# The opening of a two-layer diffusion backbone: order of its loads, context vectors by TensorE, a narrow low-rank block, squares ahead

## The reference, cut to what matters

```python
mod_x = (sc @ ada_w[l] + ada_b[l])      # sc = silu(c); scc = silu(c_ctx) for the context
sh1x, sc1x, g1x, sh2x, sc2x, g2x = split(mod_x, 6)
hx = modulate(rms_norm(x, norm1_g[l]), sh1x, sc1x)   # h * (1 + scale) + shift
gq, gkk, gv, gg, lr_f, lr_b, bq, bk, bv = split_cols(h @ w_in, EVEN_WIDTHS)
```

## Time and profile before

| | |
|---|---|
| median of three runs | 1530.45 us (1528.8 to 1530.65) |
| profiled execution | 1528.42 us, span 1526.5 us |
| granted TensorE clock, mean | 0.998 |
| TensorE busy | 97% of the span |
| VectorE, ScalarE, GpSimd busy | 66%, 44%, 43% |

### The profile page before, as it was taken

The page is one execution under the profiler, slowest core; times in us unless marked ns, Lnnn a source line. Parts: engine busy times, 40 slices in busy tenths (PEclk is TensorE's granted clock), DMA queues, the critical chain, the costliest instruction groups (busy, mean ns, idle before and its releaser), DMA issues.

```text
span 1526.5 us, 26643 instructions
## 1 busy us (share of the span) xinstructions
PE 1478.6 (97%) x10374; PEld 1265.1 (83%) x10374; DVE 1010.6 (66%) x1534; ACT 679.2 (44%) x1171; POOL 657.7 (43%) x445
## 2 busy tenths in 40 slices
PE   6999999989999999999999999999999999999997
PEld 3888864468898989999898999855568998998996
DVE  4898877569888656466667655767636655456465
ACT  4745325562333424334242544245535464545365
POOL 0031026602556334343434433355645665556472
PEclk9999999999999999999999999999999999999999
DMA  9532110045224233243546211100013324224222
GB/s 375 213 123 93 43 42 1 2 168 178 84 87 149 83 116 106 83 139 121 196 137 219 96 60 59 67 29 2 1 50 103 102 85 132 73 93 133 93 94 84
DMA packets 51676, 157.07 MB, mean 103 GB/s; under 512 B 5568, under 2 KB 13120, under 8 KB 50016
## 3 DMA queue, kind: packets, MB, share of 16 engines
q1 hardware_dynamic: 51120, 155.17, 29.8%
q0 software_dynamic: 432, 0.20, 0.1%
HBM read 153.38 MB, written 2.10 MB: 102 GB/s over the span
## 4 chain that ended last, share of the span: by engine, by line
PE 61%; DVE 9%; issue 3%; ACT 2%; POOL 2%; DMA 1%; DVEq 0%; POOLq 0%; ACTq 0%; SPq 0%
PE psum L3391 30%; PE psum L3418 16%; PE psum L2804 5%; DVE product L1849 2%; PE psum L3075 2%; PE psum L2880 1%; PE psum L3350 1%; DMA adr_late<-adat_dram 1%; DVE bf L2394 1%; PE psum L3043 1%; DVE bf L2384 1%; DVE osb L2108 1%; PE psum L3363 1%; DVE mx L2004 1%; PE psum L2974 1%
## 5 line engine op out<-in xcount | busy, mean ns | idle before, releaser
L1150 POOL TENSOR_TENSOR flow<-fraw,fhi 128x512 fp32r<-128x512 f32 x168 | 228.6, 1380 | 96.8 <-ACT fhi L1580 90.2
L3418 PE MATMUL psum<-gated,fhi 128*128 128x512 f32 (+1 forms) x1032 | 254.2, 355 | 3.2 <-DVE xT L2503 2.3
L1580 ACT ACTIVATE fhi<-fraw 128x512 fp32r<-128x512 f32 (+1 forms) x272 | 163.5, 614 | 181.4 <-POOL fraw L1136 88.0
L2804 PE MATMUL psum<-act,whi 128*128 128x512 f32 (+1 forms) x1008 | 215.6, 332 | 0.1
L1156 POOL TENSOR_TENSOR flow<-fraw,fhi 128x512 fp32r<-128x512 f32 (+1 forms) x96 | 123.2, 1300 | 175.3 <-ACT fhi L1580 174.7
L3418 PEld LDWEIGHTS psum<-gated,fhi 128*128 128x128 f32 x1032 | 169.2, 188 | 32.6 <-issue 2.8
L3391 PE MATMUL psum<-tlo,fhi 128*128 128x384 f32 (+1 forms) x608 | 187.9, 309 | 0.0
L3391 PE MATMUL psum<-thi,fhi 128*128 128x384 f32 (+1 forms) x608 | 187.8, 309 | 0.0
L2804 PEld LDWEIGHTS psum<-act,whi 128*128 128x128 f32 x1008 | 153.9, 189 | 20.8 <-issue 2.3
L3418 PE MATMUL psum<-gated,flow 128*128 128x512 f32 (+1 forms) x516 | 154.5, 355 | 0.0
L2503 DVE SCALAR_TENSOR_TENSOR xT<-psum,mod,xT 128x512 f32<-128x512 f32 (+1 forms) x141 | 87.8, 655 | 97.8 <-PE psum L3418 97.7
(11 more groups left out here) (287 smaller groups left out, 3320.6 us busy)
## 6 DMA issues: line engine op xcount, KB each, us to landing
fraw<-weights_dram SPq DMA_DIRECT2D x88, 512.0 KB, 3.5
adr_late<-adat_dram SPq DMA_DIRECT2D x49, 512.0 KB, 4.6
raw<-weights_dram SPq DMA_DIRECT2D x44, 512.0 KB, 3.5
fraw<-weights_dram SPq DMA_DIRECT2D x64, 256.0 KB, 2.7
adr<-adat_dram SPq DMA_DIRECT2D x26, 512.0 KB, 4.6
ada_w<-ada_dram SPq DMA_DIRECT2D x8, 1024.0 KB, 13.6
fraw<-weights_dram SPq DMA_DIRECT2D x32, 192.0 KB, 2.4
xT<-x_in_dram SPq DMA_DIRECT2D x3, 1024.0 KB, 16.8
```

The lines of the kernel that those rows point to most:

```text
L1150: nc.gpsimd.tensor_tensor(low_piece(L, j, x), weight_piece(L, j, x), high_piece(L, j, x).bitcast(F32), ALU.subtract).then_inc(sem("f_lo"), 1)
L1580: A(high_piece(L, j, x)[:, 0:cols], source, ACT.Copy).then_inc(sem("f_hi"), 1)
L2804: last = MM(out_[:, o:o + t1 - t0], w_, a_[:, t0:t1], start=k == order[0] and j == 0, stop=k == order[-1] and j == 2)
L3418: last = MM(ps, w_, a_[:, t0:t1], start=k == 0 and i == 0, stop=k == nk - 1 and i == 2)
```

## The change

The scale weights are the first that SP issues; params and the identity are issued by ScalarE, the other constants come later. The context tokens are loaded behind all eight halves of ada_w, and GpSimd's three loads wait for them. The places of ada_w move, so that cb is free from the start: it is filled at the opening from 16 products of the activated vectors, spread over 128 columns, with the identity (`c_spread`), by two copies. Block 0 keeps only its 32 low-rank columns in memory, in the transfer and in the products. TensorE multiplies constants six times before the first work and six times before block 0 (`warmed`). The squares of x are taken in holes of ScalarE's order and added before the context's, which follow the context's inputs; the mean square stands within block 1. In the linear attention two semaphores become one. The table for Ln and Exp is loaded at the start, not ahead of the root.

```diff
+LOW_RANK = 32
+WARMING = 6
...
-        ada_w = at("ada_w", [P, ADA_RING, 4, 512], E)
+        ada_w = [at(f"ada_w{i}", [P, 4, 512], o) for i, o in enumerate((G, G + 8192, G + 16384, E + 24576))]
...
+        def block_columns(n):
+
+            return KT * LOW_RANK if n == 0 else BLOCKS[n]["nk"] * P
+
+        def block_rows(n):
+
+            return slice(0, LOW_RANK if n == 0 else P)
...
-            sp.dma_start(par[:, :], params).then_inc(sem("s_par"), 16)
-            sp.dma_start(con[:, CC_ID:], consts[:, CC_ID:]).then_inc(sem("s_con"), 16)
...
             sp.dma_start(xT[:, half:KT, 0:NX], x_tiles[:, half:KT, 0:NX]).then_inc(sem("s_xb"), 16)
-            sp.dma_start(xT[:, :, NX:T], x_tiles[:, :, NX:T]).then_inc(sem("s_xc"), 16)
             for h in range(ADA_RING, 2 * len(ADA_EARLY)):
                 load_ada(h)
-            sp.wait_ge(sem("s_adamm"), 5)
-            load_c()
+            sp.dma_start(xT[:, :, NX:T], x_tiles[:, :, NX:T]).then_inc(sem("s_xc"), 16)
+            sp.dma_start(con[:, CC_ONES:], consts[:, CC_ONES:]).then_inc(sem("s_con"), 16)
             sp.dma_start(stage[:, :], weights[RING, :, :]).then_inc(sem("s_stage"), 16)
             sp.dma_start(gkw[0:32, :], gkw_in).then_inc(sem("s_rope"), 16)
-            sp.wait_ge(sem("s_adamm"), 7)
             load_late(0)
...
+            pool.wait_ge(sem("s_xc"), 16)
             pool.dma_start(bandb[:, :], masks).then_inc(sem("s_idr"), 16)
...
+            act.dma_start(par[:, :], params).then_inc(sem("s_par"), 16)
+            act.dma_start(con[:, CC_ID:CC_ONES], consts[:, CC_ID:CC_ONES]).then_inc(sem("s_con"), 16)
             act.wait_ge(sem("s_par"), 16)
             act.wait_ge(sem("s_cpad0"), 1)
             A(cpad[:, :, 0:2], par[:, PC_C:PC_C + 16].rearrange("p (k c) -> p k c", c=2), ACT.Silu) \
                 .then_inc(sem("s_cpad"), 1)
+            nc.scalar.preload_act_table_set(LN_EXP)
+            for c in range(2):
+                act.wait_ge(sem("s_cbm"), c + 1)
+                last = A(cb[:, c, :], c_out[c], ACT.Copy)
+            last.then_inc(sem("s_cb"), 1)
             ada_copy(0)
             high(0)
-            for k in range(KT):
-                if k % 4 == 0:
-                    act.wait_ge(sem("s_modA"), 2 if k else 1)
-                    act.wait_ge(sem("s_xb" if k else "s_xa"), 16)
-                A(act_tile("proj", 0, k, 0)[:, 0:NX], xT[:, k, 0:NX], ACT.Copy, scale=modA[:, 0, k, 0:1]) \
-                    .then_inc(sem("s_nhx"), 1)
-                if k == 3:
-                    high(1)
-                    high(2)
-                    ada_copy(1)
+            act.wait_ge(sem("s_modA"), 1)
+            act.wait_ge(sem("s_xa"), 16)
+            for k in range(KH):
+                input_first(k, 0)
+            high(1)
+            high(2)
+            for k in range(KH):
+                first_square(0, k)
+            ada_copy(1)
+            act.wait_ge(sem("s_modA"), 2)
+            act.wait_ge(sem("s_xb"), 16)
+            for k in range(KH, KT):
+                input_first(k, 0)
+            first_square(0, KH)
+            first_square(0, KH + 1)
+            ada_copy(2)
+            first_square(0, KH + 2)
+            first_square(0, KH + 3)
+            ada_copy(3)
             act.wait_ge(sem("s_xc"), 16)
-            for k in range(KT):
-                A(act_tile("proj", 0, k, 0)[:, NX + 2:TX], xT[:, k, NX:T], ACT.Copy, scale=modA[:, 0, k, 1:2]) \
-                    .then_inc(sem("s_nhh"), 1)
-            for k in range(KT):
-                if k == 4:
-                    ada_copy(2)
-                square(0, k, T)
-            def c_activated(times):
-                act.wait_ge(sem("s_cbl"), 16 * times)
-                A(cb[:, :, :], cb[:, :, :], ACT.Silu).then_inc(sem("s_cb"), 1)
-
-            ada_copy(3)
-            c_activated(1)
+            input_first(0, 1)
+            input_first(1, 1)
             act.wait_ge(sem("s_mod"), 4)
             shifts_high(NORM[0]).then_inc(sem("s_shift"), 1)
+            for k in range(2, KT):
+                input_first(k, 1)
+            for k in range(KT):
+                first_square(1, k)
             root(0, T)
...
             for h in range(2):
                 ada_reduce(h)
                 dve.wait_ge(sem("s_mod"), h + 1)
-                mod_scale(0, 4 * h, 4 * h + 4)
+                mod_scale(0, KH * h, KH * h + KH)
                 if h == 0:
                     weights_low(0)
                 dve.wait_ge(sem("s_modA"), h + 1)
-                for k in range(4 * h, 4 * h + 4):
-                    hi, lo = [act_tile("proj", 0, k, low) for low in range(2)]
-                    dve.wait_ge(sem("s_nhx"), k + 1)
-                    STT(out=lo[:, 0:NX], in0=xT[:, k, 0:NX], scalar=modA[:, 0, k, 0:1], in1=hi[:, 0:NX].bitcast(F32),
-                        op0=ALU.mult, op1=ALU.subtract).then_inc(sem("s_nlx"), 1)
+                for k in range(KH * h, KH * h + KH):
+                    first_low(k, 0)
                 if h == 0:
                     weights_low(1)
                     weights_low(2)
-            for k in range(KT):
-                hi, lo = [act_tile("proj", 0, k, low) for low in range(2)]
-                dve.wait_ge(sem("s_nhh"), k + 1)
-                STT(out=lo[:, NX + 2:TX], in0=xT[:, k, NX:T], scalar=modA[:, 0, k, 1:2],
-                    in1=hi[:, NX + 2:TX].bitcast(F32), op0=ALU.mult, op1=ALU.subtract).then_inc(sem("s_nhl"), 1)
-            for k in range(KT):
-                if k == 1:
-                    dve.wait_ge(*nq("sq", 0, 1))
-                if k == 4:
+                if h == 1:
                     ada_reduce(2)
-                add_square(0, k, T)
+                for k in range(max(1, KH * h), KH * h + KH):
+                    first_add(0, k)
             ada_reduce(3)
+            first_low(0, 1)
+            first_low(1, 1)
             dve.wait_ge(sem("s_shift"), 1)
             shifts_low(NORM[0]).then_inc(sem("s_shift"), 1)
+            for k in range(2, KT):
+                first_low(k, 1)
+            for k in range(1, KT):
+                first_add(1, k)
...
-                        .then_inc(sem("g_am2"), 1)
-                    dve.wait_ge(sem("g_am"), pr + 1)
-                    dve.wait_ge(sem("g_am2"), pr + 1)
+                        .then_inc(sem("g_am"), 1)
+                    dve.wait_ge(sem("g_am"), 2 * pr + 2)
...
-                    wh_, wl_ = whi[:, n, k * P:k * P + P], wlo[:, n, k * P:k * P + P]
+                    r = block_rows(n)
+                    w = r.stop
+                    wh_, wl_ = whi[:, n, k * w:k * w + w], wlo[:, n, k * w:k * w + w]
                     for j, (w_, a_) in enumerate(((wh_, hi_), (wh_, lo_), (wl_, hi_))):
-                        last = MM(out_[:, t0:t1], w_, a_[:, t0:t1], start=k == 0 and j == 0,
+                        last = MM(out_[r, t0:t1], w_, a_[:, t0:t1], start=k == 0 and j == 0,
...
+                pe.wait_ge(*nq("sqadd", q, 2 * KT - 2 if q == 0 else KT - 1))
...
+            def warmed(times):
+
+                for _ in range(times):
+                    MM(lin[0][:, 0:512], part64[:, :], part64[:, :].unsqueeze(1).to_broadcast([P, 4, P]), start=True,
+                       stop=True)
+
+            def c_spread(c):
+
+                for k in range(KT):
+                    last = MM(c_out[c][:, k * P:k * P + P], cpad[:, k, c:c + 1].to_broadcast([P, P]), ident, start=True,
+                              stop=True)
+                last.then_inc(sem("s_cbm"), 1)
+
+            pe.wait_ge(sem("s_cpad0"), 1)
+            warmed(WARMING)
             pe.wait_ge(sem("s_cpad"), 1)
             pe.wait_ge(sem("s_con"), 16)
+            for c in range(2):
+                c_spread(c)
             ada_mm(0)
             ada_T(0)
+            warmed(WARMING)
             first_blocks(0, 0, range(0, 4))
+            pe.wait_ge(sem("s_cb"), 1)
+            first_blocks(1, 0, range(0, 4))
             ada_mm(1)
-            first_blocks(1, 0, range(0, 2))
+            first_blocks(2, 0, range(0, 2))
             ada_T(1)
-            first_blocks(1, 0, range(2, 4))
-            first_blocks(2, 0, range(0, 4))
+            first_blocks(2, 0, range(2, 4))
             first_blocks(0, 0, range(4, 8))
             ada_mm(2)
             first_blocks(1, 0, range(4, 6))
...
             first_blocks(2, 0, range(4, 6))
             ada_T(3)
             first_blocks(2, 0, range(6, 8))
+            first_blocks(0, 1)
+            first_blocks(1, 1, range(0, 4))
             mean_square(0, T)
-            for n in range(3):
-                first_blocks(n, 1)
+            first_blocks(1, 1, range(4, 8))
+            first_blocks(2, 1)
```

More of the change, by code:

```diff
@@ L1271, in input_high, with input_first, c_activated @@
                 last.then_inc(sem("s_nhh"), 1)
+            def input_first(k, part):
+                a, b = ((0, NX), (NX, T))[part]
+                A(act_tile("proj", 0, k, 0)[:, a + 2 * part:b + 2 * part], xT[:, k, a:b], ACT.Copy,
```

(42 more changed lines are left out.)

30 lines of the change are left out of this document (17 added, 13 removed).

## The result

| | before | after |
|---|---|---|
| median of 8 runs each, us | 1530.55 (1528.8 to 1532.85) | 1535.74 (1533.09 to 1536.52) |
| profiled execution, us | 1528.42 | 1535.99 |
| its span, us | 1526.5 | 1534.2 |
| fourth weight block starts, us | 53.92 | 60.34 |

The kernel became slower: the medians differ by 5.2 us, the means by 4.6, and the ratio of the runs is 1.0027 (95% interval 1.0018 to 1.0037, which is 2.8 to 5.7 us). The forecast was 1531.05; the time is that of the rival "the identity lands late" (1536), and lies 0.2 us above the high end of the range, an end that came from that rival and not from the forecast's own sum (1529 to 1533).

The account below looks back on a forecast made before the run. TensorE, busy 97% of the span, was taken as the bound. Fourth block +1.0 us, less 0.2 for weight loads and up to 0.3 for a wait, gave +0.6: median 1531.05 us, own range 1529 to 1533, with rivals 1526.2 to 1535.5.

Parts of the forecast that it names:

- the identity lands late: Slower rival, opening: identity lands at 7 to 8.8 us beside the scale weights, +4.8 to +6.6, middle 1536 us; chance 0.17.
- Transfers of the scale weights: Opening: issued first, scale halves 0 and 1 land at 5.9 and 8.6 us instead of 7.9 and 10.5.
- Params and identity on ScalarE's queue: Opening: params land between 2.7 and about 4.5 us, identity between 4.0 and about 8.8, taken as 4.9.
- Spreads: 16 added context-vector products before the first scale product: 6.9 or 3.5 us by clock, their end taken as 10.1 us.
- From there to the first product: Spreads' end to first block product: scale product 2.0 us plus chain 3.7, so 5.7 us, first product at 15.8.
- TensorE's work to the end of the fourth transposes: From first block product: 23.4 us of work plus two new waits of 0.3 and 1.1, 24.8 us.
- Behind the fourth transposes: Until the fourth block: VectorE's in-order chain takes 14.3 us against 11.2 of TensorE's own work, adding 3.1 of waiting.
- forecast second wait: TensorE wait ahead of the fourth block, about half of the 3.1 us behind the fourth transposes.
- Sum: Fourth block starts at 54.9 us against 53.92, +1.0; less small gains, +0.6 us.
- Behind the fourth block: From fourth block to the end: TensorE is the bound, so its shift carries to the end one for one.
- the gains booked at 0.5 us: 0.2 us for fewer weight loads, up to 0.3 for one wait less per pair in the linear attention's masking.
- The tail stays under TensorE: Faster rival: VectorE's chain behind the fourth transposes shrinks to 11.2 us, fourth block at 50.4, -4 us, 1526.4; chance 0.21.

Follow-up runs that it names:

- e7_no_spread: Changed kernel without the 16 spread products and ScalarE's two copies; context vectors loaded as 1 MB late, identity awaited only at the transposes: 1530.98 us.
- e8_act_alone: Changed kernel, but SP holds its first transfer until the identity, still issued by ScalarE, has landed: 1530.79 us.
- e1_sp_first: Changed kernel with params and the identity issued by SP ahead of the scale weights, not by ScalarE: 1528.81 us.
- e2_ms_later: Changed kernel with the mean square behind all of block 1's context products, not in their middle: 1535.15 us.
- e6_context_early: e1_sp_first with context tokens loaded before scale halves 4 to 7, their parts and most squares before the fourth transposes, mean square behind block 0's context products: 1526.42 us.
- e4_no_warm: Changed kernel without both sets of six warming products: 1538.4 us.
- e9_context_act: Changed kernel with e6_context_early's edits of the context and the mean square; params and identity still issued by ScalarE: 1531.0 us.
- e10_early_no_warm: e6_context_early without both sets of warming products: 1529.52 us.
- e11_halves_4_5_first: e6_context_early with scale halves 4 and 5 loaded ahead of the context tokens, 6 and 7 behind: 1530.16 us.

## Why the prediction was off

- *Transfers of the scale weights* (forecast 5.9 and 8.6 us): 6.02 and 8.67 in `e7_no_spread`. This was right.
- *Params and identity on ScalarE's queue*: this step failed. Params landed at 6.35 us, outside the bounds of 2.7 to 4.5, and the identity at 9.1, beyond the far bound of 8.8, where I took 4.9. I had chosen the hardware queue's row over GpSimd's, on the ground that GpSimd issues by another path. But the con row of SP was a transfer that stood ahead of the 1 MB ones in their own queue, and the identr row one with 1 MB transfers of another queue beside it. What made the difference was this company (`e8_act_alone`: 2.2 us alone), not the path. The near row was the one taken under the same load. The far bound itself was too early: the 8.8 us of identr run from its issue, so a bound from that row is 1.2 + 8.8 = 10 us, and the measured 9.1 lies inside it.
The rule cited of the Trainium skill ("DMA: Bandwidth & Descriptors", "Queues, rings and completion order": a DMA engine takes turns between queues packet by packet) goes with this: 7.9 us beside, 2.2 alone.
- *Spreads*: 32 instructions in 5.39 us, between the bounds of 3.5 and 6.9 and as sized (5.2). Their end came at 14.5 instead of 10.1: 4.2 from the landing, 0.2 from the length. The size came out, its reason did not: the prediction held that the clock could not have had its five microseconds without a gap. In `e1_sp_first` TensorE had worked for only 2.9 us when the spreads followed, and they took 3.89 us, nearly all at the high level.
- *From there to the first product*: 5.8 us, forecast 5.7. The scale product took 1.92 (2.0).
- *TensorE's work to the end of the fourth transposes*: 24.6 us, forecast 24.8; its two new waits 0.24 and 0.98, forecast 0.3 and 1.1. This was right.
- *Behind the fourth transposes*: 15.4 us, forecast 14.3. The mechanism was right, VectorE's chain in order, and the wait ahead of the mean square was there (2.01, forecast about 1.5). Missing was the clock: after that wait mean square to root took 4.12 us instead of 3.27. The forecast second wait, ahead of the fourth block, did not appear; I take it that TensorE's own products at the low clock filled it. In `e2_ms_later` (2.32 us) and `e8_act_alone` (0.55) it did appear.
- *Sum*: 4.4 + 0.1 - 0.2 + 1.1 = 5.4 us on top of the forecast 54.9, hence 60.3; measured 60.34.
- *Behind the fourth block*: between the two profiles the shift carried on (6.4 at 60 us, 6.6 to 300 us), and the gains booked at 0.5 us were not seen. To the times it did not carry one for one: 6.4 us became 5.2 between medians and 4.6 between means. Two things in the record go that way. The profiled execution of before ran 2.1 us under its median. And the landing in the profile of after (9.1 us) is the latest of the five profiles with the same transfers on ScalarE's queue, whose earliest is 7.7 (`e2_ms_later`). The fourth block of one profile tells the time of a kernel to about 2 to 3 us here.
- *Rivals*: "the identity lands late" gave the mechanism and its turning point (a landing at 5.3). That its 1536 came so close is in part luck: it had neither the 1.1 us of the tail's clock nor the loss between profile and medians, and the two nearly cancel. Its chance of 0.17 was too low, given that one of the two rows of small transfers showed it. "The tail stays under TensorE" named the true remedy: `e6_context_early` does that, and ran in 1526.42. The rival's 1526.4 is luck: its fourth block was to start at 50.4 and started at 51.91.

## What to carry to other kernels

Whoever moves a small transfer that the first instruction needs should ask what will be in flight beside it, and take its price from a row with the same company. A second issuing engine saved 0.9 us of issue here and lost 5 us of landing (9.1 against 4.1 in `e1_sp_first`); first in the same queue as the large ones, the same two cost no more than the 0.98 us that the second scale half is waited for in `e1_sp_first`. And work taken out of an engine's holes and put behind the last input becomes the tail: count what VectorE must do, in order, between the last input's arrival and TensorE's next need.

## What the runs showed of the hardware

- Beside 1 MB transfers of another queue, 87.5 KB took 4.4 to 5.6 us to land and 64 KB 6.5 to 7.9 (kernel after, `e2_ms_later`, `e4_no_warm`, `e7_no_spread`, `e9_context_act`); with nothing large beside them 1.9 and 2.2 (`e8_act_alone`); ahead of them in one queue 2.0 and 1.9 to 2.9 (`e1_sp_first`, `e6_context_early`).
- A single wait of TensorE of 2.0 to 2.3 us after dense work was followed by the 1.2 GHz level (kernel after, `e1_sp_first`, `e2_ms_later`, `e4_no_warm`, `e7_no_spread`, `e8_act_alone`), as were those of 2.46 us in `e4_no_warm` and `e10_early_no_warm` and of 2.78 us in `e11_halves_4_5_first`; waits of about 1.0 us were not (`e6_context_early`, `e9_context_act`), nor were those of 1.59 and 1.74 us in `e8_act_alone`. The Trainium skill, "TensorE: Matmul & The Clock Gate", "Part 1: The HAM clock gate", describes a fall of the clock after idling, but after longer idling than these waits; the waits measured here decide. Priced in the kernel after, mean square to root took 0.85 us longer.
- The same 32 instructions took 3.9 to 4.7 us straight behind six warming products (`e1_sp_first`, `e6_context_early`, `e8_act_alone`, `e11_halves_4_5_first`), 5.2 to 5.4 with a hole of 3.4 to 4.8 us between (`e2_ms_later`, `e9_context_act`, kernel after), and 6.4 to 6.5 without warming (`e10_early_no_warm`, `e4_no_warm`).
